# Strassen products, a five-bank ring and an accumulating DMA in the second MLP matmul of a two-layer encoder step

## The reference, cut to what matters

```python
def sq_relu_ffn(h, w1, w2):
    return jnp.square(jax.nn.relu(h @ w1)) @ w2          # w1 (1024, 4096), w2 (4096, 1024)

# in reference(), for each layer i (p = prompt, s = the eight streams):
    x_p = x_p + gt1_p[:, None, :] * m_p                  # m: output of the mixer
    f_p = sq_relu_ffn(modulated_norm(x_p, norm2_g[i], sh2_p, sc2_p), ffn_w1[i], ffn_w2[i])
    x_p = x_p + gt2_p[:, None, :] * f_p                  # the same for x_s with its own gate rows
```

## Time and profile before

| | us |
|---|---|
| median of 3 runs | 3046.67 (3043.01 to 3048.01) |
| the profiled execution | 3041.4, its span 3039.7 |
| mean granted TensorE clock in it | 0.975 |
| TensorE busy | 2835.4 (93% of the span) |
| VectorE, GpSimd, ScalarE busy | 1600.2 (53%), 1114.0 (37%), 878.9 (29%) |
| MLP of layer 0 | about 1060 to 1899 us of the span |
| MLP of layer 1 | about 2240 us to the end |

### The profile page before, as it was taken

One profiled execution on the slowest core, in us unless ns is written; L12 is line 12 of the kernel. 1 busy time (PEld: TensorE's weight loads), 2 busy tenths in 40 slices (PEclk: granted clock), 3 DMA queues, 4 the chain that ended last, 5 costly groups with the idle time before them and its releaser, 6 DMA issues.

```text
span 3039.7 us, 47545 instructions
## 1 busy us (share of the span) xinstructions
PE 2835.4 (93%) x16238; PEld 2521.6 (83%) x16238; DVE 1600.2 (53%) x2720; ACT 878.9 (29%) x2007; POOL 1114.0 (37%) x1028
## 2 busy tenths in 40 slices
PE   7787888689996999999999999999999999999999
PEld 4766767588885888989898997888889998989898
DVE  4476676545554645455555556323565545454544
ACT  3255555334442221111111122323221111112121
POOL 1112101046661035454544546100015445453636
PEclk9899999889997999999999999999999999999999
DMA  5212111231215352212121214314551111111111
GB/s 211 87 59 85 60 41 68 73 91 63 66 46 180 126 180 72 80 63 88 61 90 61 90 61 144 109 42 124 174 188 48 41 41 41 41 41 41 41 41 62
DMA packets 111469, 252.66 MB, mean 83 GB/s; under 512 B 14756, under 2 KB 64836, under 8 KB 108040
## 3 DMA queue, kind: packets, MB, share of 16 engines
q1 hardware_dynamic: 107608, 238.47, 23.3%
q0 software_dynamic: 3760, 12.98, 1.3%
HBM read 220.73 MB, written 30.68 MB: 83 GB/s over the span
## 4 chain that ended last, share of the span: by engine, by line
PE 58%; issue 5%; DMA 2%; POOL 2%; DVE 1%; SPq 1%; ACT 0%; POOLq 0%; DVEq 0%; ACTq 0%
PE psum L102 19%; PE psum L104 19%; PE psum L103 19%; POOL half_acc L2230 1%; DMA half_raw<-in_w 1%; PE psum L149 1%; PE psum L2635 1%; SPq L126 1%; DMA half_w_raw<-in_w_o 0%; DMA gate_raw<-in_cm_w_in 0%; PE psum L2646 0%; DVE half_w_lo L2288 0%; PE psum L2609 0%; PE psum L2540 0%; DMA half_m<-scratch_mixT 0%
## 5 line engine op out<-in xcount | busy, mean ns | idle before, releaser
L2230 POOL TENSOR_TENSOR half_acc<-half_acc,half_upd 128x512 f32<-128x512 f32 x576 | 806.5, 1437 | 824.2 <-DVE half_upd L2355 765.0
L2355 DVE TENSOR_TENSOR half_upd<-psum,half_gates 128x512 f32<-128x512 f32 x576 | 392.7, 688 | 265.8 <-PE psum L104 231.6
L102 PE MATMUL psum<-half_hT_hi,half_w_hi 128*128 128x384 f32 x1536 | 513.7, 334 | 0.0
L104 PE MATMUL psum<-half_hT_hi,half_w_lo 128*128 128x384 f32 x1536 | 513.5, 334 | 0.0
L103 PE MATMUL psum<-half_hT_lo,half_w_hi 128*128 128x384 f32 x1536 | 513.3, 334 | 0.0
L102 PE MATMUL psum<-half_w_hi,half_s_hi 128*128 128x512 f32 x1152 | 453.0, 393 | 9.6 <-DVE half_s_lo L2348 5.1
L103 PE MATMUL psum<-half_w_lo,half_s_hi 128*128 128x512 f32 x1152 | 449.8, 390 | 0.0
L104 PE MATMUL psum<-half_w_hi,half_s_lo 128*128 128x512 f32 x1152 | 449.4, 390 | 0.0
L2342 DVE TENSOR_TENSOR half_sq<-half_relu 128x384 f32<-128x384 f32 x192 | 106.8, 556 | 486.9 <-ACT half_relu L2028 486.7
L102 PEld LDWEIGHTS psum<-half_hT_hi,half_w_hi 128*128 128x128 f32 x1536 | 288.3, 188 | 1.2
L103 PEld LDWEIGHTS psum<-half_hT_lo,half_w_hi 128*128 128x128 f32 x1536 | 288.3, 188 | 1.2
(11 more groups left out here) (354 smaller groups left out, 5116.3 us busy)
## 6 DMA issues: line engine op xcount, KB each, us to landing
half_raw<-in_w SPq DMA_DIRECT2D x128, 512.0 KB, 4.8
half_mod_w<-in_ada_w_ffn SPq DMA_DIRECT2D x32, 768.0 KB, 4.3
patt_mod_w<-in_ada_w_att SPq DMA_DIRECT2D x16, 1024.0 KB, 4.9
half_m<-scratch_mixT SPq DMA_DIRECT2D x18, 512.0 KB, 5.0
scratch_x_res<-half_x SPq DMA_DIRECT2D x18, 512.0 KB, 2.6
half_acc<-scratch_x_res SPq DMA_DIRECT2D x6, 1536.0 KB, 12.3
satt_lT_raw<-in_cacheT SPq DMA_DIRECT2D x32, 256.0 KB, 3.0
satt_l_raw<-in_cache POOLq DMA_DIRECT2D x32, 256.0 KB, 3.0
```

The costliest lines, as they stand in the source:

```text
L102: pe.matmul(out, a_hi, b_hi, start=first, stop=False)
L104: return pe.matmul(out, a_lo, b_hi, start=False, stop=last)
L2230: pool.tensor_tensor(part, part, a.upd[:, v % UPDS, :], ALU.add).then_inc(a.added, 1)
L2355: dve.tensor_tensor(a.upd[:, v % UPDS, :], psum[:, F_BANK + v % F_BANKS, :], a.gates[:, int(t == SAMPLE), half * 512:half * 512 + 512], AL ...
```

## The change

In slabs 0 to 13 of each layer (`FAST` = 14) the output stage works on pairs of token tiles: tile j of `FIRST` = (0, 1, 2, 6) with tile j of `SECOND` = (3, 4, 5, 7). A pair's outputs are the 2 x 2 block product (two token tiles x two hidden blocks) times (two hidden blocks x two column halves), and it is formed by seven block products instead of eight (Strassen's scheme in Winograd's form). Each block product is one `mm3` of three matmuls of 512 columns. Sums of the operands have to be formed and split: four of `w2` per slab (`w2_sums`, VectorE, each 128 x 512), four of s per pair (`sums_012` on VectorE for the three first pairs together, `sums_3` on GpSimd for the fourth pair, with one more for the ninth tile). The ninth tile (the streams) keeps plain products, but both its blocks and a combination share `eighth`.

The seven products of a pair are accumulated over the slabs unmixed, in `acc` [128, 4, 7, 512]. Four of the seven are added there by VectorE straight from PSUM (`read`), three are copied by ScalarE into one of two `upd` buffers (`evict`) and added by GpSimd (`add`). The banks are a ring of five. In slab 0 both engines copy into `acc` directly. After slab 13 GpSimd (`join`, 16 additions of 128 x 512) and VectorE (`merge`, two additions and one multiplication by the gate per pair) turn the products into outputs. Slabs 14 and 15 use the plain outputs of before, with four banks and two `upd` buffers.

The residual is no longer loaded: the projection steps store x to the place of the result (`x_mid` or `y`), and after slab 15's last addition to a tile GpSimd issues an accumulating DMA of the tile onto it. The gating mixer therefore reads its first two tiles back from DRAM, with scale and shift tables of their own. The gates are loaded after slab 13. Weights of the modulation come in four loads of 384 KB a slab (`mod_part`), behind the two `w1` loads on SP's list. `w1` is loaded when the hidden stage ends, `w2` when the output stage ends. The hidden units alternate between the two blocks, and relu and square work in place on parts of `s012`, `s3` and `s8`. The SBUF kept for GpSimd's DMA descriptors falls from 16384 to 4096 bytes per partition.

```diff
+SCRATCH_BYTES = 4096
+ARENA = 128 + SCRATCH_BYTES + 4 * P + 4 * KT * 32
-F_BANKS, UPDS = 3, 3
+F_BANKS, UPDS = 4, 2
+RING = (2, 3, 4, 5, 0)
+PAIRS = TT // 2
+FIRST, SECOND = (0, 1, 2, 6), (3, 4, 5, 7)
+FACTORS = {P1: (A11, B11), P2: (A12, B21), P3: (S4, B22), P4: (A22, T4), P5: (S1, T1), P6: (S2, T2), P7: (S3, T3)}
+JOBS = (P1, P6, P2, P3, P7, P4, P5)
+READ, EVICTED = JOBS[0::2], JOBS[1::2]
+N_READ, N_EVICT, N_JOBS = 4 * PAIRS + 2, 3 * PAIRS, 7 * PAIRS + 2
+PLAIN = 2
+FAST = SLABS - PLAIN
+ORDER = ([t for pair in zip(FIRST, SECOND) for t in pair] + [SAMPLE], list(range(TT)))
 ...
 # tensor
+            def free_bank(a, s, n):
+                j, place = n // 7, n % 7
+                if place % 2:
+                    pe.wait_ge(a.evicted, s * N_EVICT + (3 * j + place // 2 + 1))
+                else:
+                    pe.wait_ge(a.read, s * N_READ + (4 * j + place // 2 + 1))
+
+            def seven(a, s, j):
+                if a.makes_mod:
+                    mod_part(a, s, j)
+                pe.wait_ge(a.s_ready, s * N_S + (j + 1))
+                for place, product in enumerate(JOBS):
+                    n = 7 * j + place
+                    if n >= len(RING):
+                        free_bank(a, s, n - len(RING))
+                    s_slot, w_slot = FACTORS[product]
+                    product_of(a, bank_of(n), j, s_slot, w_slot, True, True).then_inc(a.f_ready, 1)
 ...
 # scalar
+            def evict(a, s, j, first):
+                for m, product in enumerate(EVICTED):
+                    n = 7 * j + JOBS.index(product)
+                    act.wait_ge(a.f_ready, s * N_JOBS + (n + 1))
+                    if first:
+                        out = a.acc[:, j, product, :]
+                    else:
+                        act.wait_ge(a.added, s * N_EVICT + (3 * j + m + 1 - UPDS))
+                        out = a.upd[(3 * j + m) % UPDS][:]
+                    act.activation(out, psum[:, bank_of(n), :], ACT.Copy).then_inc(a.evicted, 1)
+
+            def out_evicts(a, s, first):
+                evict(a, s, 0, first)
 ...
+                split_s(a, s, 3)
+                split_s(a, s, PAIRS)
+                evict(a, s, 1, first)
+                split_next_w1(a, s, 0)
+                evict(a, s, 2, first)
+                split_next_w1(a, s, 1)
+                evict(a, s, 3, first)
 ...
 # gpsimd
+            def sums_3(a, s):
+                x, x8 = a.s_raw[3], a.s_raw[PAIRS]
 ...
+                pool.wait_ge(a.sq_ready, s * U + U)
+                step.run(pool.tensor_tensor(x[:, S1, :], x[:, A21, :], x[:, A22, :], ALU.add))
+                step.then(pool.tensor_tensor(x[:, S3, :], x[:, A21, :], x[:, A11, :], ALU.subtract))
+                step.then(pool.tensor_tensor(x8[:, 2, :], x8[:, 0, :], x8[:, 1, :], ALU.add))
+                step.run(pool.tensor_tensor(x[:, S2, :], x[:, S1, :], x[:, A11, :], ALU.subtract))
+                pool.tensor_tensor(x[:, S4, :], x[:, A12, :], x[:, S2, :], ALU.subtract).then_inc(a.sum3_ready, 1)
 ...
+                if n // V == PLAIN - 1 and v % 2 == 1:
+                    t = v // 2
+                    pool.wait_ge(a.added, ADDED + n + 1)
+                    pool.wait_ge(a.x_stored[t % 2], 16 * ((TT + 1 - t % 2) // 2))
+                    pool.dma_start(layer_io[a.layer][1][t], a.rows(t), accum_op=ALU.add).then_inc(a.stored[min(t, 2)], 16)
 ...
+                sums_3(first, s)
+                for n in range(N_EVICT):
+                    add(first, s, n)
+            join(first)
 ...
 # vector
+            def merge(a, step, j):
 ...
+                if j < PAIRS:
+                    dve.wait_ge(a.joined, 4 * j + 4)
+                    step.run(dve.tensor_tensor(a.acc[:, j, P5, :], a.acc[:, j, P5, :], a.acc[:, j, P6, :], ALU.add))
+                    rest = a.acc[:, j, P3:P7 + 1:P7 - P3, :]
+                    step.run(dve.tensor_tensor(rest, rest, a.acc[:, j, P5:P5 + 1, :].to_broadcast([P, 2, 512]), ALU.add))
+                    gate = a.gates[0][:].unsqueeze(1).to_broadcast([P, 2, D])
 ...
+                dve.tensor_tensor(acc, acc, gate, ALU.mult).then_inc(a.merged, 1)
 ...
+            def outputs(a, s, first):
+                read(a, s, 0, first, range(3))
+                split_s(a, s, 3)
+                read(a, s, 0, first, range(3, 4))
+                read(a, s, 1, first, range(2))
+                split_s(a, s, PAIRS)
+                read(a, s, 1, first, range(2, 4))
+                read(a, s, 2, first, range(1))
+                split_w1(a, s + 1, 0)
+                read(a, s, 2, first, range(1, 4))
+                split_w1(a, s + 1, 1)
+                read(a, s, 3, first)
+                read_8(a, s, first)
+                if a.makes_mod:
+                    finish_mod(a, s)
```

774 lines of the change are left out of this document (485 added, 289 removed).

## The result

| | time, us (median; range) | profiled execution's span |
|---|---|---|
| kernel before | 3047.3 (3043.0 to 3050.6, 4 runs) | 3039.7 |
| changed kernel | 3084.7 (3082.4 to 3087.8, 4 runs) | 3082.8 |

The ratio is 1.0124, 95% interval [1.0107, 1.0142]: the change makes the kernel 1.2% slower. The forecast was 3037.5 us, with a range of 3000 to 3072.

The account below looks back on a forecast made before the run. PE was taken as the bound, busy 93% of the span. Terms -76.2 + 22 + 13 + 20 + 10 + 9 - 7 = -9, stepped from the median of 3046.67 us, gave 3037.5 us; range 3000 to 3072.

Parts of the forecast that it names:

- The matmuls removed: Output stages of 14 slabs, two layers: 96 matmuls for 108, each worth its full 0.227 us, -76.2 us.
- Layer 1's banks: Layer 1's slabs 1 to 13: PE waits for a bank before product 11, 1.7 us a slab, 22 us.
- Layer 0, 1.0 us a slab: Layer 0's steady slabs: PE waits 1.0 us before pair 1 for the second modulation load, 13 us in all.
- The 32 small matmuls stay: Layer 0's slabs: the modulation's small matmuls remain, at 0.87 us for each of two stretches.
- Slab 14, 10 us a layer: POOL's joins and DVE's merges delay the first output 4.6 us and the output stage 5 us; 20 us in all.
- With 0.5 us each: Slab 14's hidden stage: some ten DVE instructions each lose 0.5 us meeting POOL; first output 4.6 us late.
- Slab 15, layer 1: POOL's additions, waits and issues take 3.6 us a tile and set the end, with a 4 us DMA: +10 us.
- Slab 15, layer 0: Layer 0's last slab: nine issues and waits of 1.1 us come nearly wholly on top of POOL's work: +9 us.
- In layer 0 POOL already paces the last slab: Layer 0's slab 15: POOL's additions of 1.95 us set the pace before the change; basis of the +9 us.
- What goes: Slab 0: without the load of x, w2 is split before it is wanted, -7 us.
- The rival that gave 3084 us: POOL bounds every output stage, deciding from 1.49 us per addition; at 1.75 us, +37 us; chance 0.18.
- The dear DMA: Slab 15: issuing an accumulating DMA holds POOL 3 us, 43 us more, 3080 us; decides from about 1 us; chance 0.10.

Follow-up runs that it names:

- the run with all edits: Changed kernel with two evictions fewer, modulation loads ahead of w1, slab 15's residual added early, plain SP stores, layer 0's last loads reordered: 3026.4 us, ratio 0.9950.
- All cures that were tried together: Changed kernel with those edits, joins on DVE, gating last, a third weight buffer, and plain stores leaving layer 0's residual out: 2994.7 us (one run).

## Why the prediction was wrong

By its own steps:

- **The matmuls removed, -76.2 us:** right. With the stalls gone the stage is 96 x 0.227 us to the hundredth.
- **Layer 1's banks, 1.7 us a slab:** the place, the chain, 0.46 us a sum, and PE's 1.55 us (forecast 1.6) were right; with the restart (0.3 us) and 0.2 us at product 26 it is 2.1 us. +5.5 us in 13 slabs.
- **Layer 0, 1.0 us a slab:** the gap is 0.69, and 0.9 with its restart. The step that failed is "The 32 small matmuls stay (0.87 us for each of the two stretches)", which puts the split from two groups into four at nothing: in two groups they cost 26.56 - 24.52 = 2.0 us a slab, in four 2.85 (0.56 in the hidden stage, 24.09 - 21.80 in the output stage, from the run with all edits). That is 0.8 us in 13 slabs, and slab 1 is once 2.9 us longer, whose cause stays open: +12.6 us in all.
- **Slab 14, 10 us a layer:** measured 17.6 and 18.5. "With 0.5 us each" was the failing term in the hidden stage: DVE's squares, splits and short merges wait 1.0 to 1.1 us each (the two gatings 0.5), and the stage is 8.7 us longer for 4.6. Without the joins that loss is gone in layer 1. Here the rule of the Trainium skill that I had beside my own figure (SBUF — State Buffer, "Who interferes with whom": the shared port pair is an exclusive lock) was the better one; the trace agrees, 1646 for 556 ns. I had used it for the chain in front of product 11 and not for slab 14, where ten instructions meet. The same section says that a GpSimd instruction that only writes doesn't contend: the two squares that met writes took 0.56 us, which agrees. In the output stage I set DVE's work against PE's and took 5 us for what measured 9.8 more than in a steady slab before. What failed there is that DVE and POOL were taken to work side by side; the trace shows them waiting for each other through two buffers (4.09 us of POOL in each merge, 4.2 us of DVE) and colliding where they meet (3.6 us of DVE). How much of the 9.8 us is turns and how much collisions no run tells apart; a third buffer gives back 1.7 and 0.8 us only, and with POOL out of the slab altogether the stage is 27.2 us.
- **Slab 15, layer 1, 10 us:** 13.2. POOL's 3.7 us a tile were right (3.6 forecast), though made up otherwise: its additions are 1.53 us in the mean for 1.26, and the accumulating DMA lands in 5.3 us for the 4 I took. The formula of the Trainium skill that I cited (DMA: Bandwidth & Descriptors, "Anatomy of one DMA — SWDGE (gpsimd) path") gave 3.2 us; the measurement decides. A plain store by POOL lands in 2.9 us here.
- **Slab 15, layer 0, 9 us:** 22.4, the worst term. The step that failed is "In layer 0 POOL already paces the last slab"; no transfer was looked at. POOL itself waited 13.5 us for DVE's outputs between its additions, and ACT 41.1 us for gating weights. PE stood 7.95 us for modulation weights that SP had queued behind five loads of 512 KB (three of gating weights, two tables), and the accumulating stores took 27 us of the DMA engines where SP moved another 7.5 MB. All cures that were tried together bring the stretch from 84.2 to 73.9 us; the cause of the rest stays open.
- **What goes, -7 us:** right (-11.8 with two slabs' matmuls, forecast -12.4).

The terms sum to -9, the trace to +43: of the 52 us between, 18 are in the steady slabs, 16 in slab 14 and 17 in slab 15. The rival that gave 3084 us had the number and not the mechanism: POOL never paced a steady stage (18.9 of 23.9 us busy, 1.37 us an addition, for the 1.49 from which it decides). The dear DMA costs POOL 0.88 us, below the 1 us from which it was to decide; it is dear on the DMA engines instead.

## What to carry to other kernels

When work moves between DVE and POOL, count every meeting of a DVE instruction with two SBUF inputs and a reading POOL instruction at up to the whole of the other, and look at who hands buffers to whom. In the steady stage the lone durations of both sides came to 21.6 of 21.8 us, and moving an instruction only moved the stall; what helped was a form with one SBUF input (PSUM straight into the tile: 0.69 us for 0.6 + 1.3). Such a sum is a warning and no forecast: in slab 14 it came out right with additions that ran elsewhere. A seldom executed stage, the last slab or the one that unpacks, needs the same account as the steady one, with its transfers: here slabs 14 and 15 of the two layers took back 72 us, where the matmuls removed are worth 76. A load that PE waits for belongs ahead of the loads that nobody waits for yet: worth 11.5 us in the steady slabs, though only 2.7 us of the last slab's 7.3.

## What the runs showed of the hardware

- An accumulating DMA of 512 KB, SBUF to DRAM, takes POOL 0.88 us to issue (plain 0.58), lands in 5.3 us (plain 2.9) and costs the 16 engines 3.0 to 3.3 us (27.2 and 29.5 us for nine; plain 1.3). Into SBUF nine of them cost the 16 engines 25 us, 2.8 us each; while they ran alone the engines were full at 204 GB/s.
- POOL's memset of 128x512 takes 0.53 us, its copy 0.65, its addition 1.27. A DVE square of 128x384 (0.56 us alone) loses nothing beside the first, 0.04 to 0.29 us beside the second and 1.09 us beside the third, on two, four and four instances.
